# The samples of the even layer inside its output projection, and another order in the fronts of both output projections

## The reference

```python
def rwkv_step(s, inp):                       # even layer, each sample has one such step
    r_t, w_t, k_t, v_t, a_t, b_t = inp
    sa = jnp.einsum('bhvk,bhk->bhv', s, a_t)
    s = s * w_t[:, :, None, :] + sa[..., None] * b_t[:, :, None, :] + v_t[..., None] * k_t[:, :, None, :]
    return s, jnp.einsum('bhvk,bhk->bhv', s, r_t)

# end of the even layer
y = ((y - mu) * lax.rsqrt(var + GN_EPS)).reshape(bsz, t, D_A) * gn_g + gn_b      # per head of 64
y = y + (jnp.sum(r_h * k_h * r_k, -1, keepdims=True) * v_h).reshape(bsz, t, D_A) # "bonus"
out_a = y * jax.nn.silu(gate_a)
y_b = jax.nn.gelu(y_s5 + d_skip * u); y_b = y_b * jax.nn.sigmoid(y_b @ glu_w + glu_b)
out_b = y_b * jax.nn.silu(gate_b)
out = jnp.concatenate([out_a, out_b], axis=-1) @ w_out

# end of the odd layer
o_d = o_d * lax.rsqrt(jnp.mean(o_d * o_d, -1, keepdims=True) + RMS_EPS) * gn_g
out = jnp.concatenate([o_c * jax.nn.silu(g_c), o_d * jax.nn.silu(g_d)], axis=-1) @ w_out

x = layer_norm(DEEPNORM_ALPHA * x + out, ln_g[l], ln_b[l])   # after either layer
```

## Time and profile before

| | us |
|---|---|
| median of 3 runs (3340.97 to 3343.16) | 3343.15 |
| the profiled execution | 3348.46 |
| its span | 3346.7 |
| TensorE busy | 2911.9 |
| VectorE busy | 2182.6 |
| first DMA of the samples' stage (es) | 1210.45 |
| first DMA of the even output stage (oe) | 1266.65 |
| last DMA issue of oe | 1606.9 |
| first DMA of the odd output stage (oo) | 3105.17 |

### The profile page before, as it was taken

The page is one execution under the profiler, slowest core; times in us unless marked ns, Lnnn a source line. Parts: engine busy times, 40 slices in busy tenths (PEclk is TensorE's granted clock), DMA queues, the critical chain, the costliest instruction groups (busy, mean ns, idle before and its releaser), DMA issues. The chain is left out here.

```text
span 3346.7 us, 70729 instructions
## 1 busy us (share of the span) xinstructions
PE 2911.9 (87%) x27987; PEld 2413.4 (72%) x27987; DVE 2182.6 (65%) x3336; ACT 1260.0 (38%) x2269; POOL 825.8 (25%) x726
## 2 busy tenths in 40 slices
PE   8799999978998925999699999988878998987698
PEld 7699999966777724778588778766756666667476
DVE  9526556547676644786438777703448899886587
ACT  1015555434444413353011011101107888874332
POOL 4100000012232312111211111103116676664221
PEclk9899999988999967999799999999989999999899
DMA  5524544453443526563548999955531101006542
GB/s 177 204 81 147 160 148 147 144 158 97 115 107 93 123 77 186 151 178 100 204 142 279 347 332 348 331 179 166 171 126 52 64 2 64 14 19 189 196 145 90
DMA packets 470755, 506.50 MB, mean 151 GB/s; under 512 B 200017, under 2 KB 363202, under 8 KB 465162
## 3 DMA queue, kind: packets, MB, share of 16 engines
q1 hardware_dynamic: 372426, 338.16, 33.5%
q10 hardware_dynamic: 89040, 147.01, 12.7%
q0 software_dynamic: 8960, 16.81, 1.7%
HBM read 360.74 MB, written 141.31 MB: 150 GB/s over the span
## 5 line engine op out<-in xcount | busy, mean ns | idle before, releaser
L2614 POOL TENSOR_TENSOR sp_att<-sp_beta,sp_left 128x512 f32<-128x512 f32 (+3 forms) x320 | 318.3, 1005 | 197.2 <-DVE sp_left L2570 185.6
L102 PE MATMUL po_acc<-po_x_high,po_w_low 128*128 128x412 f32 (+1 forms) x840 | 306.4, 365 | 36.1 <-POOL po_w_low L95 16.9
L102 PE MATMUL pe_acc<-pe_x_high,pe_w_low 128*128 128x412 f32 (+1 forms) x840 | 305.2, 363 | 21.8 <-DVE pe_x_low L95 14.7
L103 PE MATMUL po_acc<-po_x_low,po_w_high 128*128 128x412 f32 (+1 forms) x840 | 298.5, 355 | 0.0
L104 PE MATMUL po_acc<-po_x_high,po_w_high 128*128 128x412 f32 (+1 forms) x840 | 298.3, 355 | 0.0
L104 PE MATMUL pe_acc<-pe_x_high,pe_w_high 128*128 128x412 f32 (+1 forms) x840 | 295.9, 352 | 0.0
L103 PE MATMUL pe_acc<-pe_x_low,pe_w_high 128*128 128x412 f32 (+1 forms) x840 | 295.6, 352 | 0.0
L2570 DVE TENSOR_TENSOR_SCAN sp_left<-sp_z,sp_left,sp_zero 128x512 f32<-128x512 f32 x192 | 235.4, 1267 | 13.6 <-ACT sp_z L2514 11.6
L2301 DVE TENSOR_TENSOR po_work<-po_work,po_q 128x1024 f32<-128x1024 f32 x128 | 177.0, 1383 | 86.2 <-DMA po_work<-in_cache_k 80.6
L102 PEld LDWEIGHTS po_acc<-po_x_high,po_w_low 128*128 128x128 f32 x840 | 162.1, 193 | 84.5 <-issue 30.3
L2506 ACT ACTIVATE sp_beta<-sp_z,sp_bias 128x512 f32<-128x512 f32 (+3 forms) x320 | 183.6, 631 | 73.7 <-PE sp_z L2445 46.3
(11 more groups left out here) (488 smaller groups left out, 7231.3 us busy)
## 6 DMA issues: line engine op xcount, KB each, us to landing
po_work<-in_cache_k SPq DMA_DIRECT2D x256, 256.0 KB, 5.0
po_work<-in_cache_v ACTq DMA_DIRECT2D x256, 256.0 KB, 4.5
scratch_ops<-pe_work SPq DMA_DIRECT2D x160, 128.0 KB, 2.0
out_z<-pe_o SPq DMA_DIRECT2D x84, 206.0 KB, 2.9
out_z<-po_o ACTq DMA_DIRECT2D x84, 206.0 KB, 4.6
pe_w<-in_w_e SPq DMA_DIRECT2D x21, 512.0 KB
po_w<-in_w_o ACTq DMA_DIRECT2D x21, 512.0 KB
rc_opx<-scratch_ops SPq DMA_DIRECT2D x16, 640.0 KB, 5.5
```

Of the source, the lines that this page charges most:

```text
L102: pe.matmul(out, ll, rh, start=start, stop=False)
L103: pe.matmul(out, lh, rl, start=False, stop=False)
L2614: pool.tensor_tensor(att[h][:, n % 3, 0:w], be[h][:, n % 4, 0:w], left[h][tile(n) % 2][:, at + 1:at + 1 + w], ALU.mult).then_inc(at_ok[h], 1)
```

## The change

The stage `even_samples` is gone. A class `EvenSamples` issues the same operations from within the even output stage. S and T lie in the ring of raw weights (`wr`), which is free once the low parts of the weights are made; the S5 drive uses the two halves of the ring one after the other, so its operations of 4096 elements become two of 2048 each, loaded by one DMA each. VectorE's work is a generator: `next(samples)` issues one slice. One slice stands behind the high part of tile 2, then three in each of iterations 1 to 5 of the loop over blocks: behind the first eviction, behind the norm, and behind the eviction of the next tile. TensorE's part stands between the two halves of tile 7, 9 and 11, in the bank of its transposes, and it waits for VectorE's copy out of that bank before the next transposes. SyncE loads before block 2, stores and loads the drives in iteration 2, and again in iterations 3 and 5.

In both output stages the fronts get another order. The loads begin with what the first norm needs (in the even stage `y_a`, in the odd one `o_d`), then four slices of weights, the maps, the rest of block 0, the other weights. ScalarE does the norm of block 0 ahead of its gates and sigmoids. TensorE does tile 0 and half of tile 1 before the means and GLU of block 1, and the sums of squares of block 1 after tile 1. GpSimd has one more slice of weights ahead of the first low part. In the odd stage the raw weights have eight buffers in place of four.

```diff
+class EvenSamples:
...
+    def sync_begin(self, sp):
+        for e in (0, 1):
+            rows, vals = slice(64 * e, 64 * e + 64), slice(32 * e, 32 * e + 32)
+            sp.dma_start(self.S[rows], self.state[:, vals, :]).then_inc(self.ready, 16)
+            sp.dma_start(self.vt[rows, :, :], self.vecs.rearrange("n b (h c) -> (b h) n c", c=64)).then_inc(self.ready, 16)
+            sp.dma_start(self.vv[rows, :], self.vecs[S_V].rearrange("b (h c) -> (b h) c", c=64)[:, vals]
+                         ).then_inc(self.ready, 16)
...
+    def sync(self, sp, b):
+        drive = lambda e: sp.dma_start(self.ub[e].rearrange("p b c -> p (b c)"),
+                                       self.u[4 * e:4 * e + 4].rearrange("(o b) c -> o (b c)", o=1).broadcast_to([P, 4 * 512])
+                                       ).then_inc(self.ub_in, 16)
+        if b == self.STATE:
+            sp.wait_ge(self.s_new, 1)
+            for e in (0, 1):
+                sp.dma_start(self.state_out[:, 32 * e:32 * e + 32, :], self.S[64 * e:64 * e + 64]).then_inc(self.s_put, 16)
+            sp.wait_ge(self.y_done, 1)
+            drive(0)
+            sp.wait_ge(self.s_put, 32)
+            drive(1)
+        elif b == self.DRIVE:
+            sp.wait_ge(self.yc_done, 4)
+            sp.dma_start(self.y_a[:, :, SEQ:COLS], self.yc[:, :, :]).then_inc(self.put, 16)
+            sp.wait_ge(self.new, 1)
+            sp.dma_start(self.mt, self.kept_m).then_inc(self.mt_in, 16)
+            sp.dma_start(self.h_out, self.hn[:, :, :]).then_inc(self.put, 16)
+        elif b == self.TURN:
+            sp.wait_ge(self.ycd, 1)
+            sp.dma_start(self.y_b[:, :, SEQ:COLS], self.ycs[:, :, :]).then_inc(self.put, 16)
+            sp.wait_ge(self.put, 48)
+    def tensor(self, pe, b):
+        if b == self.DRIVE:
+            pe.wait_ge(self.y_done, 1)
+            pe.transpose(self.tr[0:32, 0, 0:P], self.yt[:, :], self.idt[:, :]).then_inc(self.tr_done, 1)
+        elif b == self.READ:
+            pe.wait_ge(self.new, 1)
+            pe.wait_ge(self.mt_in, 16)
...
+            mm.then_inc(self.mm, 1)
+        elif b == self.TURN:
+            pe.wait_ge(self.gel, 1)
...
+            mm.then_inc(self.trd, 1)
+    def tensor_free(self, pe, b):
+        if b == self.DRIVE:
+            pe.wait_ge(self.yc_done, 4)
+        elif b == self.READ:
+            pe.wait_ge(self.pre, 1)
+        elif b == self.TURN:
+            pe.wait_ge(self.ycd, 1)
...
+    def vector(self, dve):
+        drive = lambda e: link(dve.tensor_tensor(self.ub[e], self.ub[e], lb, ALU.mult))
+        driven = lambda e: link(dve.tensor_reduce(self.bu[:, 4 * e:4 * e + 4, :],
+                                                  self.ub[e].rearrange("p b (g c) -> p b g c", c=GC), AX.X, ALU.add))
+        dve.wait_ge(self.ready, 96)
+        link(dve.tensor_tensor(T, S, row(S_A), ALU.mult))
+        link(dve.tensor_reduce(self.sa[:, :], T, AX.X, ALU.add))
+        yield
+        link(dve.tensor_tensor(S, S, row(S_W), ALU.mult))
+        yield
+        link(dve.tensor_tensor(T, col(self.sa[:, :]), row(S_B), ALU.mult))
+        yield
+        link(dve.tensor_tensor(S, S, T, ALU.add))
+        yield
+        link(dve.tensor_tensor(T, col(self.vv[:, :]), row(S_K), ALU.mult))
+        yield
+        dve.tensor_tensor(S, S, T, ALU.add).then_inc(self.s_new, 1)
+        dve.wait_ge(self.s_new, 1)
+        yield
+        link(dve.tensor_tensor(T, S, row(S_R), ALU.mult))
+        dve.tensor_reduce(self.yt[:, :], T, AX.X, ALU.add).then_inc(self.y_done, 1)
+        yield
+        dve.wait_ge(self.late, 96)
+        dve.wait_ge(self.ub_in, 32)
+        drive(0)
+        yield
+        driven(0)
+        drive(1)
+        yield
+        dve.wait_ge(self.tr_done, 1)
...
+                dve.tensor_copy(self.yc[r:r + 32, :, :], src).then_inc(self.yc_done, 1)
+        driven(1)
...
+        dve.tensor_tensor(self.hn[:, :, :], self.bu[:, :, :], self.w[:, :, :], ALU.add).then_inc(self.new, 1)
+        yield
+        link(dve.tensor_tensor(self.ur[:, :], self.ur[:, :], self.dr[:, :], ALU.mult))
+        yield
+        yield
+        dve.wait_ge(self.mm, 1)
+        dve.tensor_tensor(self.ur[:, :], self.ur[:, :], self.tr[0:NS, 0, :], ALU.add).then_inc(self.pre, 1)
+        yield
+        yield
+        yield
+        dve.wait_ge(self.trd, 1)
+        dve.tensor_copy(self.ycs[:, :, :], self.tr[:, 0, 0:4 * NS].rearrange("p (k b) -> p k b", k=4)).then_inc(self.ycd, 1)
...
-            self.wr, self.wh, self.wl = sb("w", [P, 4, D]), sb("w_high", [P, KT, D]), sb("w_low", [P, KT, D])
+            self.RING = 4 if even else KT
+            self.wr, self.wh, self.wl = sb("w", [P, self.RING, D]), sb("w_high", [P, KT, D]), sb("w_low", [P, KT, D])
...
-        load(0)
+        load_first(0, self.a_in)
...
+        for k in range(4):
+            weights(k)
         for dst, src in maps:
             sp.dma_start(dst, src).then_inc(self.cst_b, 16)
-        for k in range(4):
+        load_rest(0)
+        for k in range(4, KT):
             weights(k)
+        residual(0)
         if self.even:
             sp.dma_start(self.idt[:, :], self.const["ident"]).then_inc(self.lnc, 16)
         load(1)
-        for k in range(4, KT):
-            weights(k)
         for dst, src in ((self.g, self.gain), (self.b, self.shift)):
             sp.dma_start(dst[:, :], src.broadcast_to([P, D])).then_inc(self.lnc, 16)
-        residual(0)
         residual(1)
+        if self.even:
+            sp.wait_ge(self.w_low[0], 4)
+            sp.wait_ge(self.w_low[1], 4)
+            self.es.sync_begin(sp)
         for b in range(self.NB):
             if b + 2 <= self.NB:
                 load(b + 2)
             residual(2 * b + 2)
             if 2 * b + 3 <= TT:
                 residual(2 * b + 3)
+            if self.even:
+                self.es.sync(sp, b)
...
-        front(0)
+        centre(0)
         back(0)
-        for b in range(self.NB):
-            front(b + 1)
+        glu(0)
+        tile(0)
+        tile(1, (0,))
+        centre(1)
+        glu(1)
+        tile(1, (1,))
+        back(1)
+        turned(0)
+        for b in range(1, self.NB):
+            centre(b + 1)
+            glu(b + 1)
             tile(2 * b, (0,))
             back(b + 1)
             tile(2 * b, (1,))
             turned(2 * b - 1)
-            tile(2 * b + 1)
+            tile(2 * b + 1, (0,))
+            if self.even:
+                if b >= self.es.DRIVE:
+                    pe.wait_ge(self.yT_ok, 2 * b)
+                self.es.tensor(pe, b)
+            tile(2 * b + 1, (1,))
+            if self.even:
+                self.es.tensor_free(pe, b)
             turned(2 * b)
...
-        act.wait_ge(self.cst_b, self.CST_B)
-        front(0)
-        for k in range(4):
+        weights(0)
+        squares(0)
+        for k in range(1, 4):
             weights(k)
         back(0)
+        gates(0)
+        act.wait_ge(self.cst_b, self.CST_B)
+        sigmoids(0)
         for k in range(4, KT):
             weights(k)
-        for b in range(self.NB):
-            if b:
-                norm(2 * b - 1)
+        norm(0)
+        front(1)
+        put(0)
+        back(1)
+        put_turned(0)
+        for b in range(1, self.NB):
+            norm(2 * b - 1)
             front(b + 1)
-            if b:
-                put(2 * b - 1)
+            put(2 * b - 1)
             back(b + 1)
-            if b:
-                put_turned(2 * b - 1)
+            put_turned(2 * b - 1)
...
+        samples = self.es.vector(dve) if self.even else iter(())
         dve.memset(self.eps[:, :], GN_EPS if self.even else RMS_EPS).then_inc(self.eset, 1)
         dve.memset(self.leps[:, :], LN_EPS).then_inc(self.eset, 1)
-        dve.wait_ge(self.cst_b, self.CST_B)
         if self.even:
             centre(0, 0)
             centre(0, 1)
         weights(1)
         weights(3)
+        normed(0)
         if self.even:
             unit(0)
-        scaled(0)
+        gated(0)
         high(0)
         weights(5)
         weights(7)
-        for b in range(self.NB):
+        high(1)
+        evict(0, 0)
+        evict(0, 1)
+        spread(0)
+        if self.even:
+            centre(1, 0)
+            centre(1, 1)
+        norm(0)
+        evict(1, 0)
+        if self.even:
+            unit(1)
+        scaled(1)
+        high(2)
+        next(samples, None)
+        for b in range(1, self.NB):
             t = 2 * b
             if self.even:
                 centre(b + 1, 0)
-            if b:
-                evict(t - 1, 1)
-                spread(t - 1)
+            evict(t - 1, 1)
+            spread(t - 1)
             if self.even:
                 centre(b + 1, 1)
             high(t + 1)
-            if b:
-                norm(t - 1)
+            norm(t - 1)
             if self.even:
                 unit(b + 1)
             evict(t, 0)
+            next(samples, None)
             scaled(b + 1)
             evict(t, 1)
             spread(t)
             high(t + 2)
```

(5 more changed lines are left out.)

298 lines of the change are left out of this document (146 added, 152 removed).

## The result

The changed kernel takes 3313.14 us (median of 4 runs, 3311.09 to 3314.94), beside 3343.15 for the kernel before, timed with it (3340.97 to 3347.94): ratio 0.9915, 95% interval 0.9902 to 0.9928, or 30.0 us less. The forecast was 3302.4 with a range from 3287 to 3320. The sign and the range held, and so did the mechanism in its main lines; the gain is three quarters of the 40.8 forecast.

What follows compares the result with a forecast made beforehand. TensorE bounds steady even blocks, VectorE next; nothing overlaps in the samples' stage, and TensorE waits in both heads. Terms -56.2 - 3.9 + 14.8 + 2.8 + 1.7 = -40.8 took 3343.15 to 3302.4 us, range 3287 to 3320.

Steps and rivals of the forecast that it cites:

- The samples' stage: Separate stage ahead of the even output stage: goes as a whole, barrier included, -56.2 us.
- The even head: Even stage's first DMA to tile 2's first product: 15.2 us won at the first product, 11.3 given back, -3.9.
- Rival B: Even head: block 1's chain finds cover, so the gain stays, -15 us, total 3291.3; chance 0.10.
- Blocks 1 to 3: Even stage: the samples' slices on VectorE exceed its idle time and delay TensorE, +14.8 us.
- The pause: Block 3, even stage: TensorE waits for copies out of its transposes' bank, then runs slower, costing 2.7 us.
- The 3.2 us for a late variance: Even blocks 1 to 3: late variances delay ScalarE's gates and sigmoids, VectorE waits, 1.1 us a block, 3.2 in all.
- rival A: Even blocks 1 to 3: the slices hide in VectorE's idle time, +4 us, total 3291.6; chance 0.20.
- C: Rival for even blocks 1 to 3: nothing hides, every slice costs in full, +28 us, total 3318.3; chance 0.15.
- TensorE's own: Even stage: samples' matmuls and two small groups of transposes join an engine with no idle time, +2.8 us.
- The odd stage: Odd head: bare chain to tile 2 is 4.1 us longer, first product 2.4 earlier, net +1.7 us.
- Rival D: Even stage: pauses drop TensorE's clock to 1.2 GHz and it stays low, slower than before, 3389.6 us; chance 0.03.
- Signs: Expected in the profile: one first DMA, first product +40, tile 2 +91, blocks 35 to 43 us, odd-head wait 9.

Runs made afterwards that it cites:

- the fronts alone: New order in the fronts of both output stages, samples kept in a stage of their own as in the kernel before; 3339.69 us, ratio 1.0001.
- the best kernel: Changed kernel plus odd head's old order, even sums of squares before half a tile, copies first, drives' loads early, half the drives' work in block 4; 3292.97 us, again 3296.68.

## Why the prediction was right, and where it was off

**The samples' stage, -56.2.** As forecast, to a tenth: it is a difference of two marks of SyncE's queue in both traces.

**The even head, -3.9, measured -1.0.** The first product was forecast at +40.1 and came at +41.4, and that it came so near is partly luck. The loads let the GLU begin at +20.5, not +22.5; the GLU took 9.4, not 8.3; and VectorE's gate, put at 2.15, took 4.06, beside a GpSimd operation that began 0.34 before it (timelines of VectorE and of GpSimd):

```profile
1239.31 4.06 DVE L941 TENSOR_TENSOR oe_cat<-oe_sig,oe_gate_b 128x256 f32<-128x256 f32 x4
```

```profile
1238.97 2.52 POOL L95 TENSOR_TENSOR oe_w_low<-oe_w,oe_w_high 128x1024 fp32r<-128x1024 f32 x1 [17.37 <-ACT oe_w_high L798]
```

From there the order of steps is borne out one by one: sums of squares forecast at +72.2, measured +73.9; 3.7 us to VectorE's first use (3.8); 5.2 to its cast (5.1); the slice, 4.6, wholly bare. Mis-sized is also the end: from the slice's end to tile 2 I had 5.0 and the trace shows 6.3, since after the wait of 6.99 the second half of the GLU goes at the lower clock, 0.50 in the rows below; without the slice (the fronts alone) it follows in 3.4 after its start, here in 5.6. Rival B is refuted: tile 2 starts at +94.4, not +80, and half a tile of cover brings 6 us, which the order as made doesn't have.

On the first slice, the rows and the rule of the Trainium skill that the prediction named. The slice starts 0.17 us before the low part (timelines of VectorE and of GpSimd):

```profile
1290.61 2.29 DVE L451 TENSOR_TENSOR oe_w<-oe_w,oe_es_vec 128x2048 f32<-128x2048 f32 x1
1292.93 2.29 DVE L452 TENSOR_REDUCE oe_es_sa<-oe_w 128x32 f32<-128x2048 f32 x1
1295.25 0.69 DVE L927 SCALAR_TENSOR_TENSOR oe_cat<-oe_part,oe_cat 128x512 f32<-128x512 f32 x1
```

```profile
1290.78 4.33 POOL L95 TENSOR_TENSOR oe_cat_low<-oe_cat,oe_cat_high 128x1024 fp32r<-128x1024 f32 x1 [35.89 <-DVE oe_cat_high L90]
```

VectorE keeps its 2.29; GpSimd takes 4.33 for what takes 2.39, so it stood 1.9 us. It ended 2.2 after the first operation of the slice, during the second, which was not slowed. This agrees with the Trainium skill (SBUF — State Buffer, Who interferes with whom) in both points: who comes first keeps the shared ports for its whole instruction, and a tensor_reduce never contends for them on this chip.

**Blocks 1 to 3, +14.8, measured +16.8.** VectorE's busy time was right in sum (110.8 forecast, 109.9 measured), and the cost came out within 2.0; but the cost does not follow from that sum, as the run with the state's operations cut down shows, so this nearness is partly luck. Block 1 holds 31.92 and hides all of it; block 3 alone costs 12.7, and 10 of them also without the state's slices. What failed is the sum over three blocks against three times a block's length: I left out the wait for the drives' load, 2.36, which comes back whole when it is taken away, and priced the wait for the copies at nothing of its own. The copies stand behind both the first reduction and the second drive (4.6 us), and putting them first gives back 2 of these 4.6. The pause was forecast to cost 2.7; TensorE's busy time in block 3 is 36.51, 2.5 over a block. The 3.2 us for a late variance show as no new delay: VectorE's wait for the sigmoids is 1.31, 1.27 and 1.27 in the three blocks, and 1.30 already in the earlier trace rows; it is idle time that the slices cannot use. Rivals A (+4) and C (+28) both fell. Where A was right is block 1: VectorE's waits for the root and for the means' bank, 1.97 and 3.02 in the earlier trace rows, are gone there, and that idle time swallows 5 us.

**TensorE's own, +2.8, measured +2.6.** Block 4, with the 64 matmuls, lasts 35.94 with no idle time, and block 5 34.5.

**The odd stage, +1.7, measured +5.6: the step that was furthest off.** The first product came 1.1 earlier, not 2.4. From there the walk held up to tile 2's first product, but for 0.9: 24.4 to the sums (forecast 23.5), 7.5 from them to the low part (7.35), 2.35 for it (2.4). Then half a tile and sums were put at 7.4 and took 9.2, because products after a pause of 8.06 run slow, as they did in tile 0 of the same head, which I counted so; I counted the second pause as if it had none. So 1.8 of the miss are the second pause, 1.3 the first product and 0.9 the two tiles. The second profile of the changed kernel has the stage at +4.1, with 23.6 to the sums, so the size of the miss is good to 1 or 2 us. With the old order and all else as it is, the loss is gone.

**The clock.** Rival D fell: the granted clock is 1.00 in blocks 1, 2 and 4, and 0.89 in block 3. Busy us by stretch behind the three pauses (6.99 in the even head, 8.06 in the odd one, 10.14 in block 3), the clock third from the right:

```profile
1296.00:1299.00 3.00, 3.00 (x7) 2.46 (x8) 2.93 (x6) 1.41 (x3) 0.26 (x1) 0.50 0.47 154
1299.00:1301.50 2.50, 2.50 (x9) 2.04 (x9) 2.46 (x2) 2.49 (x4) 2.50 (x1) 0.70 0.07 28
...
3125.00:3129.00 4.00, 4.00 (x10) 3.14 (x11) 3.97 (x3) 2.90 (x3) 2.89 (x1) 0.50 0.19 77
3129.00:3133.00 4.00, 4.00 (x17) 3.30 (x16) 1.72 (x2) 1.28 (x1) 0.00 (x0) 0.87 0.84 254
...
1408.70:1414.00 5.30, 5.30 (x15) 3.46 (x16) 5.16 (x8) 2.29 (x2) 0.00 (x0) 0.58 0.19 57
1414.00:1420.00 6.00, 6.00 (x30) 5.28 (x29) 5.90 (x7) 4.67 (x6) 2.85 (x1) 1.00 0.68 195
```

Behind each, TensorE first works at 0.50, which is 1.2 GHz, and is back at 2.4 GHz some 4 to 5 us later: 2 us and a little more are lost each time. Behind short waits the price is not fixed. The same wait of 2.63 in block 2 is followed by 16 products in 3.72 at a granted clock of 1.00 in the changed kernel, in 5.18 at 0.69 with the sums of squares moved, and in 6.78 at 0.52 in the second run of the best kernel; in the latter two another wait of 1.2 stands 9 us ahead, in the first one of 0.9. What decides stays open.

**Signs.** Met are the one first DMA, the first product, the idle ahead of the transposes and, at 8.06 for 9, the wait in the odd head. Not met: the first product of tile 2 (+94.4, not +91), the even stage (18.5 longer, not 15), the blocks of 35 to 43 (34.0, 38.0 and 46.7, so that block 1 alone looks like rival A), and VectorE's idle time near nothing (2.1, 2.0 and 4.7). The missing 7.3 us of the profiled sum are 3.9 in the odd stage, 2.9 in the head, 2.0 in blocks 1 to 3, less 1.4 in unchanged parts. The profiles show 33.5 and the medians 30.0 because the profiled execution before lies 5.3 over its median (3348.46) and the one after 1.8 over its own (3314.94).
